# Three stacked transformer blocks: weights asked for one stage ahead, and block three's condition finished inside the last feed-forward step in column tiles

## The chip, the core and the metric

The kernel runs on one core of a Trainium2 chip, written directly against the five engines: TensorE (PE, matrix products, with its weight loads shown as PEld), VectorE (DVE), ScalarE (ACT), GpSimd (POOL) and SyncE (SP). SP and POOL issue transfers to 16 DMA engines that all queues share. The metric is the device time of one launch in microseconds, the median of the timed runs. All data are 32-bit floats.

## The reference, cut to what matters

Three blocks follow one another on x, 256 tokens of width 1024. Block one is attention and 32 experts; block two is a hybrid layer whose one wide input product `x @ w_in_2` has 8192 columns; block three has two layers, each of a feed-forward part, a mixer and a second feed-forward part:

```python
c_act = jax.nn.silu(c)
for i in range(2):
    mod = (c_act @ mod_w[i] + mod_b[i])[:, None, :]
    sh0, sc0, g0, sh1, sc1, g1, sh2, sc2, g2 = jnp.split(mod, 9, axis=-1)
    h = rms_norm(x, norm_g[i, 0]) * (1 + sc0) + sh0
    x = x + 0.5 * g0 * swiglu(h, ffn_w_gu[i, 0], ffn_w_down[i, 0])
    h = rms_norm(x, norm_g[i, 1]) * (1 + sc1) + sh1
    y = pool_mixer(h, pool_w, pool_scale) if i == 0 else diff_attention(h, ...)
    x = x + g1 * y
    h = rms_norm(x, norm_g[i, 2]) * (1 + sc2) + sh2
    x = x + 0.5 * g2 * swiglu(h, ffn_w_gu[i, 1], ffn_w_down[i, 1])
return rms_norm(x, final_g)
```

`swiglu(h)` is `(silu(h @ w_g) * (h @ w_u)) @ w_down` with 2816 inner columns. `mod`, the condition, is nine pieces of 1024 columns a layer.

## The kernel before

The program is a row of stages. A stage holds its tiles and semaphores, and its `block()` gives each engine its own instruction list. All engines meet at the end of a block, so a stage's first transfers are issued when the stage before has ended on every engine.

**Block two** (`second`, line 1618) multiplies w_in_2 in a ring of two slots of 512 columns. SP loads the first two slots at lines 1669 to 1670 and reloads a slot at line 1684 when its last bank is filled. Beside it `SideSums` (line 279) computes the first three pieces of layer 0's condition: POOL loads mod_w in halves of 2 MB (line 299), and DVE adds the rows up, weighted by the condition, with 16 instructions a piece (lines 268 and 272). What results has one partial sum per partition; a product with ones adds the 128 partitions up later.

**A feed-forward stage** (`ffn`, line 2067; ffn00, ffn01 in layer 0, ffn10, ffn11 in layer 1) first runs `Norm`: ACT squares, DVE scales, PE transposes (line 471), DVE and ACT write hT (lines 457, 432). Then come 11 steps of 256 inner columns. `up(s)` makes gate and up products of slot s into banks 4+2s and 5+2s (line 2132), ACT applies silu (line 2175), DVE multiplies (line 2195), `down(s)` adds to banks 0 to 3 (line 2146). Weights lie in two slots: SP loads 2 MB of gate and up weights (lines 2097, 2098) when the slot's second bank is filled, then 1 MB of down weights (line 2101) after the slot's last down product. The order on PE is written out: up 0, up 1, down 0, four turns of (up 0, down 1, up 1, down 0), up 0, down 1, down 0. `residual` (line 2214) then multiplies by the gate and adds to x on DVE. ffn00 carries six pieces of side sums, ffn01 nine; POOL's mod_w loads (2 MB each) run beside SP's weights.

**A modulation stage** (`modulation`, line 331, called by `modulation3`) follows ffn00 with two parts (mixer and second feed-forward of layer 0) and ffn01 with three. PE turns shift and scale sums into columns with 128x1 products (line 382), and gates into rows with 128x512 products (line 390). DVE adds the biases, and folds in the norm's gain, the factor 0.5 or pool_scale.

**The mixers**: `pool_mixer` (line 2226) needs 1 MB of weights; `diff_attention` (line 2308) loads 8 MB of q and k weights (wqk), small tables, lamrow last, and 4 MB of v weights at its start (lines 2338 to 2344). PE waits for wqk and all the tables before its first product (line 2370).

`third` (line 2633) calls these in order.

## Time and profile before

| | |
|---|---|
| timed runs | 3047.74 us median of 3 (3039.37 to 3050.79) |
| profiled execution | 3042.34 us, span 3040.7 us |
| PE busy | 2671.5 us, 88% of the span |
| PE weight loads busy | 1588.9 us, 52% |
| DVE, ACT, POOL busy | 783.5, 336.9, 29.7 us |
| mean granted clock of PE | 0.917 |
| read from memory | 727.83 MB, 240 GB/s over the span |

### The profile page before, as it was taken

The numbers are of one execution on the slowest core, as the hardware profiler recorded it, in microseconds if no ns is written. First come the engines' busy times: TensorE is split into PE (matmuls) and PEld (weight loads), VectorE is DVE, ScalarE is ACT, GpSimd is POOL, SyncE is SP. The second block draws the span as 40 slices with busy tenths as digits, with TensorE's granted clock in tenths as the row PEclk, the third lists the DMA queues.
The fourth block names the chain that finished last, engine by engine and source line by source line (L and its number), as shares of the span: only waits on it lengthen the run. The fifth ranks groups of instructions, "written<-read, shape, count | busy, mean of one in ns | idle before, by whom it ended". The sixth has DMA issues, their size and how long they took to land. (4 is left out here: it accounts for less than half of the span.)

```text
span 3040.7 us, 28745 instructions
## 1 busy us (share of the span) xinstructions
PE 2671.5 (88%) x10935; PEld 1588.9 (52%) x10936; DVE 783.5 (26%) x1801; ACT 336.9 (11%) x663; POOL 29.7 (1%) x48
## 2 busy tenths in 40 slices
PE   6977699999997999968999799959998996957998
PEld 3433333333332333337787477647767774734775
DVE  1222322212121221232832243234441001232001
ACT  2111011111111111110122000010001000021000
POOL 0000000000000000000000000000000000000000
PEclk8967699999999999989999899969997997967999
DMA  7600599999998899966323477347963545102443
GB/s 296 242 0 2 229 419 428 428 429 428 428 428 342 349 428 428 428 265 234 139 100 149 152 288 260 111 148 259 354 225 132 166 154 196 57 1 83 152 136 105
DMA packets 188107, 729.65 MB, mean 240 GB/s; under 512 B 9343, under 2 KB 102877, under 8 KB 159381
## 3 DMA queue, kind: packets, MB, share of 16 engines
q1 hardware_dynamic: 169044, 653.41, 54.7%
q0 software_dynamic: 19008, 75.50, 6.5%
q8 instruction: 36, 0.59, 0.1%
q14 instruction: 19, 0.15, 0.0%
HBM read 727.83 MB, written 1.05 MB: 240 GB/s over the span
## 5 line engine op out<-in xcount | busy, mean ns | idle before, releaser
L2132 PE MATMUL bank<-hT,ffn_wgu 128*128 128x256 f32 x2816 | 622.3, 382 | 29.1 <-DMA ffn_wgu<-in_ffn_w_gu 25.8
L2132 PEld LDWEIGHTS bank<-hT,ffn_wgu 128*128 128x128 f32 x2816 | 538.7, 192 | 123.1 <-issue 42.8
L1387 PE MATMUL bank<-experts_raw,tiled_xs 128*64 128x512 f32 x2112 | 474.3, 599 | 17.4 <-DMA experts_raw<-in_w_up 13.6
L1387 PEld LDWEIGHTS bank<-experts_raw,tiled_xs 128*64 128x64 f32 x2112 | 147.8, 138 | 333.3 <-issue 295.1
L2146 PE MATMUL bank<-ffn_wd,ffn_actT 128*128 128x512 f32 x704 | 308.6, 592 | 0.0
L1387 PE MATMUL bank<-experts_raw,tiled_act_s 128*64 128x512 f32 x1056 | 241.0, 602 | 48.4 <-DMA experts_raw<-in_w_down 47.1
L1714 PE MATMUL bank<-hT,second_ring 128*128 128x256 f32 x1024 | 226.1, 384 | 17.2 <-DMA second_ring<-in_w_in 17.2
L1714 PEld LDWEIGHTS bank<-hT,second_ring 128*128 128x128 f32 x1024 | 197.4, 193 | 46.1 <-issue 18.5
L2195 DVE TENSOR_TENSOR ffn_actT<-ffn_silu,bank 128x256 f32<-128x256 f32 x88 | 36.9, 421 | 694.1 <-ACT ffn_silu L2175 694.1
L2146 PEld LDWEIGHTS bank<-ffn_wd,ffn_actT 128*128 128x128 f32 x704 | 133.8, 190 | 151.3 <-issue 149.2
L1387 PEld LDWEIGHTS bank<-experts_raw,tiled_act_s 128*64 128x64 f32 x1056 | 71.3, 137 | 196.1 <-issue 123.5
L272 DVE SCALAR_TENSOR_TENSOR layer_sums<-ffn_side_w,cact,layer_sums 128x512 f32 (+1 forms) x210 | 140.6, 746 | 3.4 <-DMA ffn_side_w<-in_mod_w 3.4
L2175 ACT ACTIVATE ffn_silu<-bank 128x256 f32<-128x256 f32 x88 | 33.8, 384 | 851.6 <-PE bank L2132 851.6
L1523 DVE COPY tiled_spread<-bank 128x256 f32<-128x256 f32 x33 | 14.0, 425 | 433.9 <-PE bank L1423 433.7
L1554 DVE TENSOR_TENSOR tiled_up<-bank,tiled_cur 128x512 f32<-128x512 f32 x33 | 22.8, 692 | 252.9 <-PE bank L1407 252.9
L2370 PE MATMUL bank<-hT,diff_wqk 128*128 128x256 f32 x256 | 59.1, 392 | 16.6 <-DMA diff_lamrow<-in_diff_lambda 16.6
L1432 PE MATMUL bank<-tiled_ys,tiled_spread 64*128 64x512 f32 x264 | 65.6, 615 | 0.8 <-ACT tiled_ys L1478 0.8
L1415 PE MATMUL bank<-tiled_h_rows,tiled_choice 128*64 128x512 f32 x272 | 65.9, 606 | 0.0
L2370 PEld LDWEIGHTS bank<-hT,diff_wqk 128*128 128x128 f32 x256 | 50.5, 198 | 24.3 <-issue 16.9
L1482 ACT ACTIVATE tiled_g_rows<-bank 128x512 f32<-128x512 f32 x33 | 19.7, 598 | 293.6 <-PE bank L1387 293.6
L1938 DVE SCALAR_TENSOR_TENSOR second_pT<-second_glu,cols,second_pT 128x256 f32<-128x256 f32 x120 | 47.6, 477 | 0.0
L1485 ACT ACTIVATE tiled_u_rows<-bank 128x512 f32<-128x512 f32 x33 | 19.7, 598 | 224.9 <-PE bank L1387 224.9
(460 smaller groups left out, 1974.2 us busy)
## 6 DMA issues: line engine op xcount, KB each, us to landing
experts_raw<-in_w_gate SPq DMA_DIRECT2D x64, 2048.0 KB, 23.7
experts_raw<-in_w_up SPq DMA_DIRECT2D x64, 2048.0 KB, 25.1
experts_raw<-in_w_down SPq DMA_DIRECT2D x64, 2048.0 KB, 25.5
ffn_wgu<-in_ffn_w_gu SPq DMA_DIRECT2D x88, 1024.0 KB, 9.8
ffn_side_w<-in_mod_w POOLq DMA_DIRECT2D x30, 2048.0 KB, 12.0
ffn_wd<-in_ffn_w_down SPq DMA_DIRECT2D x44, 1024.0 KB, 5.2
second_ring<-in_w_in SPq DMA_DIRECT2D x16, 2048.0 KB, 7.7
mla_wm<-in_w_mod SPq DMA_DIRECT2D x24, 1024.0 KB, 6.4
```

What stands on the lines that cost most here:

```text
L272: op = vec.scalar_tensor_tensor(dst[:, o], src[:, j, o], c[:, j:j + 1], dst[:, o], ALU.mult, ALU.add)
L1387: last = nc.tensor.matmul(bank[b][h * HALF:(h + 1) * HALF, :], stationary(kt), raw[p][:, k, h * C:(h + 1) * C], start=kt == 0, stop=kt == ...
L1415: last = nc.tensor.matmul(bank[X][n * HALF:(n + 1) * HALF, :], choice[:, t, :], h_rows[:, t, n * C:(n + 1) * C], start=t == 0, stop=t == T ...
L1432: nc.tensor.matmul(bank[2 * t + h][:], spread[rows, t * P:(t + 1) * P], ys[rows, :], start=False, stop=False)
L1554: vec.tensor_tensor(tiles(up), turned(U), wide(cur[:, KT:2 * KT]), ALU.add).then_inc(u_taken, 1)
L1714: last = nc.tensor.matmul(bank[b][:, (f % 2) * SEQ:(f % 2 + 1) * SEQ], w_k[s][:, k, f * P:(f + 1) * P], core.hT[:, k, :], start=k == 0, st ...
L1938: op = vec.scalar_tensor_tensor(dst, src, w, dst, ALU.mult, ALU.add)
L2132: last = nc.tensor.matmul(bank[b][:, m * SEQ:(m + 1) * SEQ], wgu[:, s, m, k, f * P:(f + 1) * P], core.hT[:, k, :], start=k == 0, stop=k == ...
L2146: last = nc.tensor.matmul(bank[b][:], actT[:, s, f, t * P:(t + 1) * P], wd[:, s, f, n * 512:(n + 1) * 512], start=start and f == 0, stop=s ...
L2175: nc.scalar.activation(silu[:, b - 4, :], core.bank[b][:, 0:SEQ], ACT.Silu)\
L2195: vec.tensor_tensor(actT[:, s, f, :], silu[:, b - 4, :], core.bank[b][:, SEQ:], ALU.mult)\
L2370: last = nc.tensor.matmul(bank[q % 4][:, f * SEQ:(f + 1) * SEQ], wqk[:, k, a:a + P], core.hT[:, k, :], start=k == 0, stop=k == KT - 1)
```

## The change

Four things, all in the second and third block.

1. The ring of block two, one large tile `big` (block two's pT, then both weight slots of all feed-forward stages, then the attention's v weights and q/k), and the semaphores of their loads live across stages.
2. Loads are issued in the stage before: the first w_in slots behind the last expert weights; ffn00's first two steps in block two after `mixed`; ffn01's and ffn10's in the last step of the feed-forward stage before (`following`); wqk at ffn10's start (`early`); ffn11's in the attention after the v products. The slot order changes with the stage (`slots`).
3. The modulation stages are gone. The bias row is added by the side sums, on one partition (others zero). The last step of ffn00 and ffn01 makes, per part, the two column pieces as four rows in 32-column tiles of one bank and the gate as rows, between the last up and down product; ACT copies them out; four transposes per part turn the rows into columns; DVE finishes them. POOL applies pool_scale.
4. `ffn10` and `ffn11` keep their normalised x in the ring; so does the attention for v, probabilities and x.

```diff
+    def first_w_in_2(self, sp):
+        w_in = self.ins["w_in_2"].rearrange("(k p) n -> p k n", p=P)
+        for s in range(2):
+            sp.dma_start(self.ring[:, s, :].rearrange("p (k n) -> p k n", k=KT), w_in[:, :, s * 512:(s + 1) * 512])\
+                .then_inc(*self.slot_in[s].up())
...
-            if first and j == 0:
+            if first and j == 0 and bias is not None:
+                op = vec.scalar_tensor_tensor(dst[:, o], src[:, j, o], c[:, j:j + 1], bias[:, o], ALU.mult, ALU.add)
+            elif first and j == 0:
...
+        if self.bias is not None:
+            self.st.nc.gpsimd.memset(self.bias[:], 0.0).then_inc(*self.zeroed.up())
+            pool.wait_ge(*self.zeroed.own())
+        load_bias(slice(self.first * PIECE, (self.first + 1) * PIECE))
...
             for s in range(2):
                 pool.wait_ge(*self.w_used[s].next(pool))
+                if s == 0:
+                    load_bias(bass.ds(i * PIECE + (self.first + 1) * PIECE, PIECE))
                 load(s, bass.ds(i * PIECE + (self.first + 1) * PIECE, PIECE))
...
@@ experts_tiled, sync
             load(E - 1, 2)
+            core.first_w_in_2(sp)
@@ second, sync
-            for s in range(2):
-                sp.dma_start(w_k[s], w_in[:, :, s * 512:(s + 1) * 512]).then_inc(*slot_in[s].up())
...
+            sp.wait_ge(*S["mixed"].next(sp, 4))
+            core.ffn_weights.first_steps(sp, 0, 0)
...
+class FfnWeights:
+    def slots(layer, which):
+        return (0, 1) if which == 0 else (1, 0)
...
+    def first_steps(self, sp, layer, which):
+        for n, s in enumerate(self.slots(layer, which)):
+            self.load_gu(sp, layer, which, s, self.step(n))
+            self.load_wd(sp, layer, which, s, self.step(n))
...
@@ ffn, sync
-            for s in range(2):
-                load_gu(s, lambda o: slice(o + s * F, o + (s + 1) * F))
-                load_wd(s, lambda o: slice(o + s * F, o + (s + 1) * F))
+            if early:
+                early(sp)
...
+            if following:
+                sp.wait_ge(*core.filled[5 + 2 * B].next(sp))
+                weights.load_gu(sp, *following, B, weights.step(0))
+                sp.wait_ge(*wd_used.next(sp))
+                weights.load_wd(sp, *following, B, weights.step(0))
+                sp.wait_ge(*core.filled[5 + 2 * A].next(sp))
+                weights.load_gu(sp, *following, A, weights.step(1))
+                sp.wait_ge(*core.filled[3].ahead(2))
+                weights.load_wd(sp, *following, A, weights.step(1))
...
@@ ffn, tensor
-            up(0)
-            down(1)
-            down(0, stop=True)
...
+            up(A)
+            if finish:
+                pe.wait_ge(*side.step.next(pe, (2 * KT - 2) * side.n_pieces))
+                pe.wait_ge(*side.w_used[1].next(pe, side.n_pieces))
+            n = 0
+            for part, *_ in finish:
+                a = (3 * part - side.first) * PIECE
+                core.claim(pe, b_of(n))
+                for g in range(4):
+                    last = nc.tensor.matmul(bank[b_of(n)][32 * g:32 * g + 32, :], core.ones[:, 0:32],
+                                            sums[:, a + g * 512:a + (g + 1) * 512], start=True, stop=True)
+                last.then_inc(*core.filled[b_of(n)].up())
+                n += 1
+                for h in range(2):
+                    o = a + 2 * PIECE + h * 512
+                    core.claim(pe, b_of(n))
+                    nc.tensor.matmul(bank[b_of(n)][:], core.ones[:], sums[:, o:o + 512], start=True, stop=True)\
+                        .then_inc(*core.filled[b_of(n)].up())
+                    n += 1
+            down(B)
+            core.copied(pe, *spare_banks[:2 * len(finish)])
+            for i in range(len(finish)):
+                core.claim(pe, b_of(n))
+                for j in range(4):
+                    last = nc.tensor.transpose(bank[b_of(n)][:, j * P:(j + 1) * P], cond_rows[i][:, j * P:(j + 1) * P],
+                                               core.ident[:])
+                last.then_inc(*core.filled[b_of(n)].up())
+                n += 1
+            down(A, stop=True)
...
@@ diff_attention, sync
-            sp.dma_start(wqk[:], w[:, :, 0:2 * D]).then_inc(*qk_in.up())
...
+            for b in (6, 7):
+                sp.wait_ge(*core.filled[b].ahead(TT))
+            core.ffn_weights.first_steps(sp, 1, 1)
...
@@ third
             sums = s0.sb("sums", [P, 6 * PIECE])
-            ffn(core, 0, 0, *part(0, 0), (w[0], 3, 6, sums))
-            modulation3(core, 0, [1, 2], 3, sums)
+            ffn(core, 0, 0, *part(0, 0), (w[0], 3, 6, sums, b_row(0)), following=(0, 1),
+                finish=[(1, 0, core.gate3[1], core.ins["pool_scale_3"]), (2, 0, core.gate3[2], None)])
...
-            ffn(core, 0, 1, *part(0, 2), (w[1], 0, MODS3, sums))
-            modulation3(core, 1, [0, 1, 2], 0, sums)
-        ffn(core, 1, 0, *part(1, 0))
-        diff_attention(core, *part(1, 1))
+            ffn(core, 0, 1, *part(0, 2)[0:2], last_gate[:], (w[1], 0, MODS3, sums, b_row(1)), following=(1, 0),
+                finish=[(n, 1, core.gate3[n], None) for n in range(3)])
...
+            ffn(core, 1, 0, *part(1, 0), early=load_qk)
+            diff_attention(core, wqk, qk_in, *part(1, 1))
```

The order of instructions on SP from the last expert weights to block two, before:

```order
L1262 DMA experts_raw<-in_w_down 128x4096 x2
L175 UNCONDITIONAL_BRANCH
L1600 UNCONDITIONAL_BRANCH
L1602 DMA experts_out_post<-in_norm_ffn_post 128x1024
L175 UNCONDITIONAL_BRANCH
L1667 UNCONDITIONAL_BRANCH
L1670 DMA second_ring<-in_w_in 128x8x512 x2
```

And the same place on SP in the changed kernel:

```order
L1228 DMA experts_raw<-in_w_down 128x4096 x2
L150 DMA ring<-in_w_in 128x8x512 x2
L186 UNCONDITIONAL_BRANCH
L1569 UNCONDITIONAL_BRANCH
L1571 DMA experts_out_post<-in_norm_ffn_post 128x1024
```

The two ring loads now stand ahead of two ends of blocks. On PE, the end of ffn00, the modulation stage and the start of the pool mixer, before:

```order
L2132 MATMUL bank<-hT,ffn_wgu 128x256 x32
L2146 MATMUL bank<-ffn_wd,ffn_actT 128x512 x16
L175 UNCONDITIONAL_BRANCH
L376 UNCONDITIONAL_BRANCH
L382 MATMUL bank<-ones,layer_sums 128x1 x32
L390 MATMUL bank<-layer_sums,ones 128x512 x4
L175 UNCONDITIONAL_BRANCH
L2256 UNCONDITIONAL_BRANCH
L471 MATMUL bank<-ident,pool_xn 128x128 x16
```

And PE at the same place in the changed kernel (`big` is the weights' tile, `ffn_cond_rows` what ACT copied):

```order
L2152 MATMUL bank<-hT,big 128x256 x32
L2193 MATMUL bank<-layer_sums,ones 32x512 x4
L2200 MATMUL bank<-layer_sums,ones 128x512 x2
L2193 MATMUL bank<-layer_sums,ones 32x512 x4
L2200 MATMUL bank<-layer_sums,ones 128x512 x2
L2166 MATMUL bank<-big,ffn_actT 128x512 x8
L2208 MATMUL bank<-ident,ffn_cond_rows 128x128 x8
L2166 MATMUL bank<-big,ffn_actT 128x512 x8
L186 UNCONDITIONAL_BRANCH
L2329 UNCONDITIONAL_BRANCH
L437 MATMUL bank<-ident,pool_xn 128x128 x16
```

The 32 products of one column are gone, the four of 512 moved up, and eight products of 32 columns and eight transposes came in. ffn01 has the same with three parts.

## Rows read from the trace of the kernel before

**Rows 1.** Busy time by stretch, around the two modulation stages (first line: columns)
```profile
core 0: us, PE busy (x) PEld busy (x) DVE busy (x) ACT busy (x) POOL busy (x), PEclk, DMA share, GB/s
...
1972.00:2000.00 28.00, 19.58 (x75) 15.77 (x76) 8.35 (x20) 3.67 (x6) 0.24 (x2) 0.60 0.35 112
...
2279.00:2321.00 42.00, 31.13 (x125) 26.21 (x124) 12.48 (x31) 5.73 (x11) 0.00 (x0) 0.63 0.33 116
```

**Rows 2.** Waits of PE: line and releaser, us in total, times, longest
```profile
PE bank L2132 <- DMA ffn_wgu<-in_ffn_w_gu: 25.8, 10, 9.7
PE bank L1714 <- DMA second_ring<-in_w_in: 17.2, 2, 9.4
PE bank L2370 <- DMA diff_lamrow<-in_diff_lambda: 16.6, 1, 16.6
```

**Rows 3.** Timeline, experts' end and block two: start, length, engine, line, idle before
```profile
1301.57 5.22 SPq L1262 DMA_DIRECT2D experts_raw<-in_w_down  x2
...
1341.86 0.66 ACT L430 ACTIVATE hT<-bank 128x256 f32<-128x256 f32 x2 [0.19 <-PE bank L471]
...
1349.66 29.50 PE L1714 MATMUL bank<-hT,second_ring 128*128 128x256 f32 x128 [7.83 <-DMA second_ring<-in_w_in]
1388.57 58.15 PE L1714 MATMUL bank<-hT,second_ring 128*128 128x256 f32 x256 [9.41 <-DMA second_ring<-in_w_in]
```

**Rows 4.** Timeline, starts of ffn00, ffn01, ffn10 and ffn11
```profile
1722.80 3.68 PE L471 MATMUL bank<-ident,ffn_xn 128*128 128x128 f32 x16 [11.30 <-DVE ffn_xn L447]
1735.79 29.28 PE L2132 MATMUL bank<-hT,ffn_wgu 128*128 128x256 f32 x128 [9.32 <-DMA ffn_wgu<-in_ffn_w_gu]
...
2032.60 3.42 PE L471 MATMUL bank<-ident,ffn_xn 128*128 128x128 f32 x16 [6.08 <-DVE ffn_xn L447]
2045.68 29.64 PE L2132 MATMUL bank<-hT,ffn_wgu 128*128 128x256 f32 x128 [9.66 <-DMA ffn_wgu<-in_ffn_w_gu]
...
2318.93 1.93 ACT L432 ACTIVATE hT<-bank,cond_mod 128x256 f32<-128x256 f32 x4 [4.56 <-PE bank L471]
...
2321.23 27.87 PE L2132 MATMUL bank<-hT,ffn_wgu 128*128 128x256 f32 x128 [1.82 <-ACT hT L432]
...
2794.49 3.67 PE L471 MATMUL bank<-ident,ffn_xn 128*128 128x128 f32 x16 [6.09 <-DVE ffn_xn L447]
2799.64 29.83 PE L2132 MATMUL bank<-hT,ffn_wgu 128*128 128x256 f32 x128 [1.48 <-ACT hT L432]
```

**Rows 5.** Timeline, start of the differential attention
```profile
2556.11 3.67 PE L471 MATMUL bank<-ident,diff_xn 128*128 128x128 f32 x16 [7.16 <-DVE diff_xn L447]
...
2576.34 16.72 PE L2370 MATMUL bank<-hT,diff_wqk 128*128 128x256 f32 x64 [16.56 <-DMA diff_lamrow<-in_diff_lambda]
```

**Rows 6.** Timeline, last residual instruction of ffn00, first instruction of the pool mixer
```profile
1972.30 0.69 DVE L2223 TENSOR_TENSOR x<-x,ffn_xn 128x512 f32<-128x512 f32 x1
...
1994.06 1.06 ACT L419 ACTIVATE pool_xn<-x 128x1024 f32<-128x1024 f32 x1 [35.83 <-PEq L175]
```

**Rows 7.** Timeline, last side sums and end of ffn01, first instruction of ffn10
```profile
2245.68 9.36 DVE L272 SCALAR_TENSOR_TENSOR layer_sums<-ffn_side_w,cact,layer_sums 128x512 f32 x14
...
2251.40 14.08 PE L2132 MATMUL bank<-hT,ffn_wgu 128*128 128x256 f32 x64 [0.44 <-DMA ffn_wgu<-in_ffn_w_gu]
...
2279.97 0.69 DVE L2223 TENSOR_TENSOR x<-x,ffn_xn 128x512 f32<-128x512 f32 x1
...
2310.66 1.06 ACT L419 ACTIVATE ffn_xn<-x 128x1024 f32<-128x1024 f32 x1 [44.77 <-PEq L175]
```

**Rows 8.** Timeline: block one's 32-column products, one down product, one bank's copy
```profile
29.62 2.78 PE L548 MATMUL bank<-mla_wm,first_cpad 128*32 128x512 f32 x24 [0.95 <-ACT mla_ctx_hT L430]
...
2348.93 7.03 PE L2146 MATMUL bank<-ffn_wd,ffn_actT 128*128 128x512 f32 x16
...
1398.51 0.60 ACT L1850 ACTIVATE second_pT<-bank 128x512 f32 x1 [18.61 <-PE bank L1714]
```

**Rows 9.** Reload of block two's ring, and the stretch until it lands
```profile
1365.53 14.20 SPq L1684 DMA_DIRECT2D second_ring<-in_w_in  x2
...
1365.00:1389.00 24.00, 14.59 (x67) 12.57 (x66) 12.46 (x22) 1.80 (x3) 2.44 (x4) 0.89 1.03 395
```

More of the change, by code:

```diff
@@ L134, in __init__, with hold @@
         self.cact = sb("cact", [P, KT])
+    def hold(self, name, shape):
+        return self.ctx.enter_context(self.nc.sbuf_tensor(name, shape, F32, side="right"))
     def clear_signals(self):
@@ L279, with __init__ @@
 class SideSums:
-    def __init__(self, st, w, first, n_pieces, acc, n_turns, slot=None):
+    def __init__(self, st, w, first, n_pieces, acc, n_turns, slot=None, bias=None):
         self.st, self.rows, self.acc, self.first = st, KT // 2, acc, first
@@ L293, in __init__ @@
         self.step = st.sem("side_step")
-        self.turn = [(x, self.per_turn) for x in self.w_in + self.w_used] + [(self.step, (2 * KT - 2) * self.per_turn)]
+        self.b_row, self.bias = bias, None
+        self.b_in, self.zeroed = st.landed("side_b_in"), st.sem("side_zeroed")
+        if bias is not None:
+            self.bias = st.sb("side_bias", [P, PIECE])
+        self.loads = self.w_in + ([self.b_in] if bias is not None else [])
+        self.turn = [(x, self.per_turn) for x in self.loads + self.w_used] + [(self.step, (2 * KT - 2) * self.per_turn)]
     def gpsimd(self, pool):
@@ L2070, in ffn @@
+def ffn(core, layer, which, scale, shift, gate, beside=None, following=None, early=None, finish=()):
     nc, ins = core.nc, core.ins
-    F = 256
+    F = FfnWeights.F
     steps = DFF3 // F
+    weights = core.ffn_weights
+    wgu, wd, gu_in, wd_in = weights.wgu, weights.wd, weights.gu_in, weights.wd_in
+    A, B = weights.slots(layer, which)
     with Stage(core, f"ffn{layer}{which}") as st:
-        wgu = st.sb("wgu", [P, 2, 2, KT, F])
-        wd = st.sb("wd", [P, 2, 2, D])
         actT = st.sb("actT", [P, 2, 2, SEQ])
@@ L2084, in ffn @@
+        cond_rows = [st.sb(f"cond_rows{i}", [P, 512]) for i in range(len(finish))]
+        pool_row = st.sb("pool_row", [P, D]) if any(own is not None for *_, own in finish) else None
+        pool_row_in, raw_gate, gate_done = st.landed("pool_row_in"), st.sem("raw_gate"), st.sem("gate_done")
+        spare_banks = (4 + 2 * B, 5 + 2 * B)
+        b_of = lambda n: spare_banks[n % 2]
+        sums = beside and beside[3]
         block = st.block()
@@ L2578, in _ @@
                                   subln[:], None, ALU.mult).then_inc(*core.emptied[q].up())
-            residual(core, dve, gate, wv, step)
+            residual(core, dve, gate, junk, step)
 def final_norm(core):
@@ L2619, in _ @@
                                                ALU.mult, ALU.mult).then_inc(*done.up())
-def modulation3(core, layer, parts, first, sums):
-    ins, b_mod = core.ins, core.ins["mod_b_3_row"]
-    at = layer * MODS3
-    own = [0.5, ins["pool_scale_3"] if layer == 0 else 1.0, 0.5]
-    gain = lambda n: core.column("norm_g_3", (layer * 3 + n) * KT, KT)
-    modulation(core, f"mod3{layer}{first}",
-               [(3 * n + m, gain(n) if m else None, core.mod3[:, layer, 2 * n + m, :]) for n in parts for m in range(2)],
-               [(3 * n + 2, b_mod[(at + 3 * n + 2) * D:(at + 3 * n + 3) * D], own[n], core.gate3[n][:]) for n in parts],
-               lambda piece: core.column("mod_b_3", (at + piece) * KT, KT), first, sums)
 def third(core):
```

238 lines of the change are left out of this document (124 added, 114 removed).

## The prediction

> **What bounds the kernel now.** The table of stretches was read first, then the list of what TensorE (PE) waited for, then the timeline at each border between stages. Nearly everywhere PE is the bound: in a feed-forward step 64 instructions of the up product and 16 of the down product follow one another without a gap. The loss is at the borders. In the stretch around the first modulation stage PE is busy 19.6 of 28 us at a granted clock of 0.60, around the second 31.1 of 42 us at 0.63 [rows 1]. The waits for transfers that can be moved are 25.8 us for feed-forward weights in 10 waits, 17.2 us for block two's weights in 2, and 16.6 us at the start of the differential attention in one [rows 2]. So I price the change border by border, as the time from the last instruction that stays to the first that stays.
>
> **Block two's first weights.** The SP queue issues the last expert weights by 1301.57 + 5.22 = 1306.8 us; the change puts the first two w_in loads right behind. They are 4.2 MB, 10.6 us at the 395 GB/s of [rows 9], and block two is more than 30 us away. hT is complete at 1341.86 + 0.66 = 1342.5; in ffn10 the first product follows the last hT write by 2321.23 - 2320.86 = 0.4 us [rows 4], so here it can start at 1342.9. It started at 1349.66 [rows 3]. **Saved 6.8.**
>
> The second wait of block two is another matter. The reload of slot 0 was issued at 1365.53 and PE got it at 1388.57, 23 us later, after 9.41 us of waiting, while the DMA engines were full and moved 395 GB/s [rows 3, 9]: the side loads of mod_w from the POOL queue compete. The change takes 4.2 MB, 10.6 us of work, out of what is ahead, but PE also asks 6.8 us earlier. Net 3.8 us, so the wait falls from 9.4 to 5.6. **Saved 3.8**, the least certain term. Its ends: all of the wait, with the 2.5 us that the products behind it lose to the low clock (estimated from the 2.0 us loss found below); or nothing, with the 6.8 us above given back as a longer wait.
>
> The Trainium skill (DMA: Bandwidth & Descriptors, "Queues, rings and completion order") says that each DMA engine takes turns between its queue rows, packet by packet. With even turns the reload would get about half of the rate, land in 10.6 us and cause no wait at all. The row with its 23 us speaks against even turns here; this is the rival "no second wait" below.
>
> **First feed-forward steps.** With weights present, a stage's first up product starts 2799.64 - 2794.49 = 5.15 us after its transposes start [rows 4]. The stage ffn00 took 1735.79 - 1722.80 = 12.99, the stage ffn01 13.08 [rows 4]. **Saved 7.8 and 7.9.** ffn10 (1.82 us wait for ACT, not for weights) and ffn11 gain nothing. In ffn00 the loads now follow the "mixed" wait and run beside the output product of block two; in ffn01 they run beside the last step and the pool mixer.
>
> **Differential attention.** PE started 2576.34 - 2556.11 = 20.2 us after its transposes, held by the small tables that sat behind 8 MB of wqk [rows 5]. wqk now lands during ffn10, so 5.15 us should do: 15.1 saved. The first 64 instructions took 16.72 us against half of 27.87 at full clock [rows 4, 5], a loss of 2.8; behind a 1.48 us wait the 128 of ffn11 lose 29.83 - 27.87 = 2.0 [rows 4], so 0.8 more. **Saved 15.9.** The 8 MB go ahead of ffn10's loop loads on the SP queue. They take 21 us from the start of the stage; the first loop load is asked for after 2321.23 - 2310.66 = 10.6 us of norm [rows 4, 7] plus 14 us of up product. I cost this at nothing. Without that cover it is one wait of some us.
>
> **The modulation stages.** The first: the last residual instruction ends 1972.30 + 0.69 = 1972.99, the pool mixer's first ACT instruction is at 1994.06 [rows 6]; a stage follows another's last instruction by 0.3. Removed 20.8. The second: 2279.97 + 0.69 = 2280.66 to 2310.66 [rows 7], removed 29.7.
>
> Added instead, per part, between the last up product and the down products: four products of 32 columns of ones, two rows of 512, and later four transposes. Block one has the same 32-column form, 24 instructions (three sets of four) in 2.78 us, 0.93 a set; a full 128x512 instruction takes 7.03 / 16 = 0.44, four of them 1.76; 16 transposes take 3.67, four 0.92 [rows 4, 8]. That is 3.6 a part. PE uses two banks in turn while ACT copies each in 0.60 [rows 8] plus a handover near 0.3; against 0.88 to 0.93 per bank that hides but for some tenths, 0.5 a stage. So 2 x 3.6 + 0.5 = 7.7 and 3 x 3.6 + 0.5 = 11.3. **Saved 13.1 and 18.4.** ffn10 pays one thing back: its first 128 instructions ran at full clock (27.87) behind the modulation's products; now they follow an idle stretch, as in ffn11 (29.83), so -2.0 and **16.4** is left. The cost of a part could be higher: 4 x 0.88 instead of 0.93 if the four column tiles ran one after another (+2.6), and 3 x 0.9 if each bank waited for ACT (+2.7), 26.5 us over five parts. Nothing excludes a small gain below, but no row suggests one.
>
> The new waits. PE waits for the sums: the last piece ends at 2245.68 + 9.36 = 2255.0, PE needs it at 2251.40 + 14.08 = 2265.5 [rows 7], 10 us of slack. Behind that wait on PE are both down products, so a late piece would cost one for one. The bias makes two DVE instructions a piece longer, 0.69 us each at most [rows 6], inside the same slack. The four or six small DVE writes of the columns lie under the last down product of 7 us. The multiply by pool_scale on POOL starts when its gate is copied and has two down products, 14 us, as cover; no row here shows it, DVE's two-input instruction of half the width takes 0.69 [rows 6]. The Trainium skill (GPSIMD Engine Reference, "Elementwise — side-by-side cycle accounting") has 4.5 us for twice the width, an estimate of 2.2 us here, which changes nothing.
>
> **Sum.** 6.8 + 3.8 + 7.8 + 13.1 + 7.9 + 16.4 + 15.9 = 71.7 us. The profiled execution took 3042.3 (span 3040.7), so 2970.6. It lies 5.4 below the median of the three timed runs and between their ends, so the same may hold after.
>
> **Rivals.**
> *No second wait* in block two: the reload lands in time. The 5.6 and 2.5 us go too: 2962.5. For it: 10.6 us less transfer work. Against: the 23 us for one load.
> *The start is given back*: side loads set the pace of DMA in block two, the reload lands when it did before, less nothing. PE's 6.8 and the 3.8 are lost: 2981.2. For it: full DMA from 1365 to 1389 [rows 9].
> *Condition work in series* on PE, with the column tiles not overlapped and ACT in every bank's turn: +26.5, 2997.1. Against: the 0.93 us of [rows 8].
> *The change doesn't do what it says*: SP reaches the early loads only at the border, because it waits in order on its queue. Then 6.8 + 3.8 + 7.8 + 7.9 + 15.9 = 42.2 stay: 3012.8. Against: each wait ahead of them is on a bank that PE fills 7 us or more before the end; only the last wd load waits for the very end.
> *Slower*: side loads crowd out weights inside ffn00 and ffn01. There are 16 loop loads of gate and up weights beside them. Now the waits there are 25.8 - 9.32 - 9.66 = 6.8 in 8 [rows 2, 4]. Were each to wait the 9.41 us of block two's reload, that is 150 us: 2970.6 + 150 - 7 = 3114. It beats the gain from (71.7 + 15) / 16 = 5.4 us a load. Against: bytes, order and slack per load stay as they are; only 4 KB of bias a piece are new.
>
> **How the numbers follow.** Forecast 0.58, no second wait 0.15, start given back 0.12, condition in series 0.06, loads not early 0.06, slower 0.03. The likeliest is 2971. The low end is 2962.5 less the 6.8 us of small weight waits, 2956. The high end is 2981.2 and 10 us more, for half of the 11.4 us between the runs and a partial overlap in the condition work: 2991. The first three cases are inside, 0.85. A measurement of this kernel tells about 0.5%, 15 us, from no change. All cases but the last are faster by more than that: faster 0.96; same 0.01 for a mixture; slower 0.03.
>
> **What would show it.** Right: no stage of modulation, PE's wait for ffn weights near 7 instead of 25.8, no wait for lamrow, first products 5.1 to 5.2 us after the transposes in ffn00, ffn01 and the attention, a piece of condition work of 7 to 8 and 11 us in the last steps, and one wait of 4 to 7 us for block two's ring. Wrong: a new wait of PE for layer_sums, waits on the spare banks longer than 1 us, a wait in ffn10's first steps behind wqk, or a span above 2991.

## The result, and the profile after

| | before | after |
|---|---|---|
| timed runs | 3046.93 us median of 4 (3039.37 to 3050.79) | 2964.32 us median of 4 (2961.74 to 2967.82) |
| profiled span | 3040.7 us | 2966.3 us |
| PE busy | 2671.5 us | 2641.4 us |
| mean granted clock of PE | 0.917 | 0.931 |

The ratio is 0.9733, 95% interval 0.9711 to 0.9754. The forecast was 2971 us with a range of 2956 to 2991. The span fell by 74.4 us, where the terms of the prediction summed to 71.7.

The main waits of PE after the change, line and releaser, us in total, times, longest:

```profile
PE bank L1354 <- DMA experts_raw<-in_w_down: 47.0, 43, 14.8
...
PE bank L437 <- DVE ring L413: 20.4, 3, 7.2
PE bank L437 <- DVE ffn_xn L413: 17.7, 2, 11.4
...
PE bank L2340 <- DVE hT L2374: 13.7, 1, 13.7
...
PE bank L2152 <- DMA big<-in_ffn_w_gu: 8.8, 7, 2.3
```

The 25.8 us for feed-forward weights [rows 2] have become 8.8, and the longest of these waits 2.3 instead of 9.7. The wait for lamrow is gone. The head of the list is the experts' down weights in block one, 47.0 us against 47.1 before. In the third block what is left is mostly DVE's arithmetic, at the borders (the L413 rows) and in the mixers. The change touches neither.

The timeline of PE after the change, one row for each place named below: start, length, engine, line, tiles, shape, count, idle time before.

```profile
1343.52 29.48 PE L1683 MATMUL bank<-hT,ring 128*128 128x256 f32 x128 [1.14 <-ACT hT L396]
1375.71 55.52 PE L1683 MATMUL bank<-hT,ring 128*128 128x256 f32 x256 [2.71 <-DMA ring<-in_w_in]
...
1709.63 3.67 PE L437 MATMUL bank<-ident,ffn_xn 128*128 128x128 f32 x16 [11.41 <-DVE ffn_xn L413]
1714.79 29.86 PE L2152 MATMUL bank<-hT,big 128*128 128x256 f32 x128 [1.48 <-ACT hT L398]
...
1924.63 11.17 PE L2152 MATMUL bank<-hT,big 128*128 128x256 f32 x51
1935.73 1.06 PE L2193 MATMUL bank<-layer_sums,ones 128*32 128x512 f32 x8
1936.73 1.99 PE L2200 MATMUL bank<-layer_sums,ones 128*128 128x512 f32 x4
1938.64 1.07 PE L2193 MATMUL bank<-layer_sums,ones 128*32 128x512 f32 x8
1939.64 1.98 PE L2200 MATMUL bank<-layer_sums,ones 128*128 128x512 f32 x4
1942.40 7.11 PE L2166 MATMUL bank<-big,ffn_actT 128*128 128x512 f32 x16 [0.78 <-ACT third_gate L2238]
1949.34 1.04 PE L2208 MATMUL bank<-ident,ffn_cond_rows 128*128 128x128 f32 x8
1950.21 7.03 PE L2166 MATMUL bank<-big,ffn_actT 128*128 128x512 f32 x16
1964.41 3.67 PE L437 MATMUL bank<-ident,pool_xn 128*128 128x128 f32 x16 [7.17 <-DVE pool_xn L413]
...
1996.82 3.68 PE L437 MATMUL bank<-ident,ffn_xn 128*128 128x128 f32 x16 [6.28 <-DVE ffn_xn L413]
2002.00 29.61 PE L2152 MATMUL bank<-hT,big 128*128 128x256 f32 x128 [1.50 <-ACT hT L398]
...
2255.76 3.67 PE L437 MATMUL bank<-ident,ring 128*128 128x128 f32 x16 [7.17 <-DVE ring L413]
2260.91 29.86 PE L2152 MATMUL bank<-hT,big 128*128 128x256 f32 x128 [1.47 <-ACT hT L398]
...
2497.78 3.68 PE L437 MATMUL bank<-ident,ring 128*128 128x128 f32 x16 [7.16 <-DVE ring L413]
2502.89 16.23 PE L2446 MATMUL bank<-hT,diff_weights_wqk 128*128 128x256 f32 x64 [1.43 <-issue]
...
2725.11 29.86 PE L2152 MATMUL bank<-hT,big 128*128 128x256 f32 x128 [1.48 <-ACT hT L398]
```

Two things are read from it. The first is the lead: the start of a piece before [rows 3 to 5] minus its start after. It grows where time was won, so its steps are the measured terms. They also carry what differs between two executions: of the 0.7 us that the first step is short, 0.6 lies ahead of it, where PE began the transposes at 1338.74 instead of 1338.18.

| up to | lead | step | predicted |
|---|---|---|---|
| block two, first product | 6.1 | 6.1 | 6.8 |
| block two, end of the ring's first products | 15.5 | 9.3 | 3.8 |
| ffn00, transposes | 13.2 | -2.3 | 0 |
| ffn00, first product | 21.0 | 7.8 | 7.8 |
| ffn01, transposes | 35.8 | 14.8 | 13.1 |
| ffn01, first product | 43.7 | 7.9 | 7.9 |
| ffn10, transposes | 60.3 | 16.6 | 18.4 |
| attention, transposes | 58.3 | -2.0 | -2.0 |
| attention, first product | 73.5 | 15.1 | 15.1 |
| ffn11, first product | 74.5 | 1.1 | 0.8 |
| end | 74.4 | -0.1 | 0 |

The second is the condition inside ffn00. The last up product ends at 1924.63 + 11.17 = 1935.80, the down product starts at 1942.40: 6.6 us. The transposes between the down products add 1950.21 - 1949.34 = 0.87. That is 7.5 us, predicted 7.7, of which 0.78 is a wait that was not predicted. Four 32-column products (eight instructions) advance PE by 1936.73 - 1935.73 = 1.00 us, against 1.91 for two full rows. In ffn01 the same reading gives 10.9, predicted 11.3.

### The profile page after: what moved, and what is told of

It reads as the page before. It is cut to its first block and busy times, and to the rows that moved or that the text cites. A ratio compares the mean times of both kernels' runs of the same rounds, so it can differ in the third digit from the quotient of the medians.

```text
span 2966.3 us, 28580 instructions
## 1 busy us (share of the span) xinstructions
PE 2641.4 (89%) x10835; PEld 1557.5 (53%) x10836; DVE 779.6 (26%) x1776; ACT 345.6 (12%) x678; POOL 43.2 (1%) x67
## 5 line engine op out<-in xcount | busy, mean ns | idle before, releaser
L2152 PE MATMUL bank<-hT,big 128*128 128x256 f32 x2816 | 623.3, 383 | 14.7 <-DMA big<-in_ffn_w_gu 8.8
L2152 PEld LDWEIGHTS bank<-hT,big 128*128 128x128 f32 x2816 | 539.9, 192 | 108.9 <-issue 24.7
L2166 PE MATMUL bank<-big,ffn_actT 128*128 128x512 f32 x704 | 309.1, 592 | 1.5 <-ACT third_gate L2238 1.5
L1683 PE MATMUL bank<-hT,ring 128*128 128x256 f32 x1024 | 224.3, 382 | 3.8 <-DMA ring<-in_w_in 2.7
L2166 PEld LDWEIGHTS bank<-big,ffn_actT 128*128 128x128 f32 x704 | 133.6, 190 | 153.2 <-issue 151.3
L1683 PEld LDWEIGHTS bank<-hT,ring 128*128 128x128 f32 x1024 | 196.5, 192 | 32.5 <-issue 5.7
L285 DVE SCALAR_TENSOR_TENSOR layer_sums<-ring,cact,layer_sums 128x512 f32 (+1 forms) x210 | 140.6, 745 | 2.8 <-DMA ring<-in_mod_w 2.8
L2446 PE MATMUL bank<-hT,diff_weights_wqk 128*128 128x256 f32 x256 | 58.7, 390 | 1.4 <-issue 1.4
L2446 PEld LDWEIGHTS bank<-hT,diff_weights_wqk 128*128 128x128 f32 x256 | 50.1, 196 | 9.0 <-issue 1.8
L1907 DVE SCALAR_TENSOR_TENSOR big<-second_glu,cols,big 128x256 f32<-128x256 f32 x120 | 47.6, 479 | 0.0
## 6 DMA issues: line engine op xcount, KB each, us to landing
ring<-in_mod_w POOLq DMA_DIRECT2D x30, 2048.0 KB, 11.9
```

Source lines behind the costliest of these rows:

```text
L285: op = vec.scalar_tensor_tensor(dst[:, o], src[:, j, o], c[:, j:j + 1], dst[:, o], ALU.mult, ALU.add)
L1683: last = nc.tensor.matmul(bank[b][:, (f % 2) * SEQ:(f % 2 + 1) * SEQ], w_k[s][:, k, f * P:(f + 1) * P], core.hT[:, k, :], start=k == 0, st ...
L1907: op = vec.scalar_tensor_tensor(dst, src, w, dst, ALU.mult, ALU.add)
L2152: last = nc.tensor.matmul(bank[b][:, m * SEQ:(m + 1) * SEQ], wgu[:, s, m, k, f * P:(f + 1) * P], core.hT[:, k, :], start=k == 0, stop=k == ...
L2166: last = nc.tensor.matmul(bank[b][:], actT[:, s, f, t * P:(t + 1) * P], wd[:, s, f, n * 512:(n + 1) * 512], start=start and f == 0, stop=s ...
L2446: last = nc.tensor.matmul(bank[q % 4][:, f * SEQ:(f + 1) * SEQ], wqk[:, k, a:a + P], core.hT[:, k, :], start=k == 0, stop=k == KT - 1)
```

## The experiments

Three places were open: how much each half of the change carries, the reload wait of block two (predicted 5.6, measured 2.71), and the clock at the starts of stages.

### Each half alone

**own_start** keeps the condition inside the last steps and puts every load back to the start of its own stage.

```diff
             load(E - 1, 2)
-            core.first_w_in_2(sp)
...
-            if early:
-                early(sp)
+            weights.first_steps(sp, layer, which)
...
         def _(sp):
+            load_qk(sp)
             for i, name in enumerate(("cos3", "sin3")):
```

> The condition work stays inside the last feed-forward steps; all weights are again asked for at their own stage's start. If the gain is a sum of borders, the trace of the change says what comes back: 6.1 us at block two's first product, 6.7 at its reload and about 2.6 of low clock behind it, 7.8 at ffn00, 7.9 at ffn01, 15.6 at the attention, 46.7 in all: 3011 us, with waits for weights of 9.3 and 9.7 us in ffn00 and ffn01 and 16.6 for lamrow. If early loads and condition work hide one another (rival), less than 40 comes back, and with mod_stages the two do not add up to the 82 us between the medians.

Measured: 3005.22 us, ratio 0.9878 (0.9857 to 0.9899). Timeline of PE in this kernel:

```profile
1350.50 30.23 PE L1681 MATMUL bank<-hT,ring 128*128 128x256 f32 x128 [8.39 <-DMA ring<-in_w_in]
...
1735.95 30.34 PE L2149 MATMUL bank<-hT,big 128*128 128x256 f32 x128 [7.32 <-DMA big<-in_ffn_w_gu]
...
2018.53 3.68 PE L437 MATMUL bank<-ident,ffn_xn 128*128 128x128 f32 x16 [6.28 <-DVE ffn_xn L413]
2026.31 30.23 PE L2149 MATMUL bank<-hT,big 128*128 128x256 f32 x128 [4.11 <-DMA big<-in_ffn_w_gu]
...
2540.03 15.57 PE L2441 MATMUL bank<-hT,diff_weights_wqk 128*128 128x256 f32 x64 [15.79 <-DMA diff_lamrow<-in_diff_lambda]
```

Each wait is back at its place, but the time fell short of the 46.7 us and the 3011 us expected. The early loads are worth 0.9878 - 0.9733, 1.45% or 44 us, with some 9 of uncertainty, and 36 between the two traces. Two starts came out shorter than before the change: ffn01's first product comes 7.8 us after the transposes start, not 13.1, and ffn00's 11.0, not 13.0 [rows 4]. In both stages POOL issues its first side load 1.8 and 2.8 us behind SP's first weights, where it was 0.5 before, since the new memset and bias load stand ahead of it. That this is why the weights land sooner was not tested. Another 2.0 us are ffn10's first 128 products, 27.87 us in this trace and 29.86 in that of the change.

**mod_stages** keeps the early loads and puts the two modulation stages back. They add the bias as they did before, and the side sums leave it out.

```diff
-                finish=[(1, 0, core.gate3[1], core.ins["pool_scale_3"]), (2, 0, core.gate3[2], None)])
+            modulation3(core, 0, [1, 2], 3, sums)
...
-                finish=[(n, 1, core.gate3[n], None) for n in range(3)])
+            modulation3(core, 1, [0, 1, 2], 0, sums)
```

> Early loads stay; the two modulation stages are back and the bias rows leave the side sums. Sum of borders: 13.1 and 18.7 us come back, less 2.0 because ffn10's first products run at full clock again: 29.8 us, 2994 us. If the clock gain of ffn10 was an accident of when the stage starts (rival), its first 128 instructions take 29.8 instead of 27.9 and 31.8 us come back.

Measured: 2988.86 us, ratio 0.9828 (0.981 to 0.9846). That puts the condition's move at 0.95%, 29 us with some 9 of uncertainty, for 29.8 expected. The two spans differ by 21.4 us only; 2.9 of the rest lie ahead of block two's first product, where the kernels are the same. Timeline of PE:

```profile
2245.31 17.50 PE L413 MATMUL bank<-ones,layer_sums 128*128 128x1 f32 x96 [1.78 <-PEq L186]
2262.67 6.94 PE L421 MATMUL bank<-layer_sums,ones 128*128 128x512 f32 x12
2277.32 3.68 PE L502 MATMUL bank<-ident,ring 128*128 128x128 f32 x16 [7.71 <-DVE ring L478]
2282.48 29.73 PE L2217 MATMUL bank<-hT,big 128*128 128x256 f32 x128 [1.48 <-ACT hT L463]
```

The second expectation missed. The modulation stands right ahead of ffn10 again, but ffn10's first 128 take 29.73 us and not 27.9. What sets the length of those products is taken up under the clock, below.

The gains are also to be read from the kernel before: early loads alone (mod_stages) give 1.72%, 52 us, the condition alone (own_start) 1.22%, 37 us. Together that is 89 where both give 2.67%, 81 us. The 8 us between them are not clear of the noise, some 11 us for three ratios. The traces point the same way: own_start has ffn00's and ffn01's starts 2.0 and 5.3 us shorter than before the change, so that much of the two starts is won by either half.

### Does the column form matter

**one_group** puts all four 32-column products of a part in the same group of columns; it leaves out rows two to four of each shift and scale.

```diff
-                    last = nc.tensor.matmul(bank[b_of(n)][32 * g:32 * g + 32, :], core.ones[:, 0:32],
+                    last = nc.tensor.matmul(bank[b_of(n)][0:32, :], core.ones[:, 0:32],
```

> All four products of a set go to the first 32 columns, so rows two to four of a set are left out of the result (shift and scale of block three are wrong in part). If the column tiles of the change run side by side, a set grows from 1.07 us to 4 x 0.88 = 3.5, five sets cost 12.2 us: 2976 us. If they already ran one after another (rival), nothing changes.

Measured: 2976.84 us, ratio 0.9791 (0.9773 to 0.981). Timeline of PE in ffn00's last step:

```profile
1932.33 3.62 PE L2193 MATMUL bank<-layer_sums,ones 128*32 128x512 f32 x8
1935.88 1.99 PE L2200 MATMUL bank<-layer_sums,ones 128*128 128x512 f32 x4
```

The same eight instructions take 3.62 us in one group of columns and 1.07 in four. Over five parts that is 12.8 us, and the ratio rose by 0.6%, 18 us, with some 9 of uncertainty. So the first half of the rival "condition in series", 2.6 us a part, was a real price, and the column groups are what avoids it. Its other half, a wait for ACT at each bank, is absent from the timeline of the change, but for the 0.78 us.

**no_bias** leaves the condition's bias out of the sums.

```diff
-            ffn(core, 0, 0, *part(0, 0), (w[0], 3, 6, sums, b_row(0)), following=(0, 1),
+            ffn(core, 0, 0, *part(0, 0), (w[0], 3, 6, sums, None), following=(0, 1),
...
-            ffn(core, 0, 1, *part(0, 2)[0:2], last_gate[:], (w[1], 0, MODS3, sums, b_row(1)), following=(1, 0),
+            ffn(core, 0, 1, *part(0, 2)[0:2], last_gate[:], (w[1], 0, MODS3, sums, None), following=(1, 0),
```

> The bias of block three's condition is left out: no bias rows, no memset, the first side-sum instruction one-input again. ffn01 loses 4.5 us to waits for weights in the change against 2.7 before. If the small bias loads on the POOL queue are the reason, the waits fall to 2.7 and the time by about 2 us. If it is the moment at which the side loads start (rival), they stay near 4.5 and the time within 1 us of the change.

Measured: 2957.78 us, ratio 0.9733 (0.9711 to 0.9755), the same as with the bias. ffn01's four weight waits came to 3.7 us, against 4.5 with it, 2.7 before the change and 2.1 in mod_stages. The bias rows cost nothing that can be told; where ffn01's 2 us went stays open.

### The small waits that were left

**after_again** and **after_third** are the changed kernel unedited, on the chips of the second and the third group of runs.

> The changed kernel once more, unedited, as the measure for the three runs beside it: 0.9733 of the time of the kernel before. It also tells how far the rows move without any edit: the first 128 gate and up products of a stage take 27.9 us where the granted clock came back to full before them and 29.9 us where it came back after they had begun, and which of the two a stage gets may differ from the first profile (29.9 in ffn00, 29.6 in ffn01, 29.9 in ffn10, 29.9 in ffn11).

> The changed kernel a third time, beside the two runs that follow, so that they are compared on one chip: 0.973 of the kernel before, as twice before (0.9733 and 0.9728).

Measured: 0.9728 (0.9714 to 0.9743) and 0.975 (0.9733 to 0.9767); medians 2964.24 and 2965.42 us.

**copied_first** moves one wait.

```diff
             up(A)
+            core.copied(pe, 4 + 2 * B, 5 + 2 * B)
...
-            down(B)
+            down(B, wait=False)
```

> In both feed-forward steps that hold the condition, the wait for the last down product's two banks stands ahead of the condition's products instead of behind them. My theory: the 0.78 and 0.73 us that TensorE waits there for ScalarE's copy of a condition tile are an accident of how evictions are counted (the counter takes in the tile's copies) and not a need, so both rows go and nothing else moves: 1.5 us less, a ratio of 0.9728. The rival: the down product's own banks were emptied late too, and a wait for VectorE of about the same length takes the place: 0.9733, no change.

Measured: 2960.79 us, ratio 0.973 (0.9716 to 0.9743). In the trace the down product follows the condition without a gap:

```profile
1942.51 1.98 PE L2202 MATMUL bank<-layer_sums,ones 128*128 128x512 f32 x4
1944.33 7.03 PE L2167 MATMUL bank<-big,ffn_actT 128*128 128x512 f32 x16
```

Both rows are gone and no other wait came in their place. 1.5 us is below what the ratio can tell.

**reload_first** holds the third block's later side loads until the reload has landed.

```diff
+        if self.hold is not None:
+            pool.wait_ge(*self.hold)
         with turns(pool, self.n_pieces - 1, *[(x, 1) for x in self.loads + self.w_used]) as i:
...
+        side.hold = slot_in[0].ahead(2)
```

> In block two the third and later pieces that GpSimd loads for the third block's condition are held until the reload of the first slot has landed. My theory: the reload lands late (16.3 us after its issue, TensorE 2.71 us idle) because it shares the DMA engines with these pieces; held back, they leave the reload to land within about 10 to 12 us, before the other slot's products end, so the wait of 2.71 us goes, and the clock does not fall there; VectorE's side work comes some 15 us later and still ends long before it is read. 3 to 5 us less than the changed kernel (0.9717 to 0.9723). The rival: the two packets before it are already in flight and carry the delay, or the clock's dip comes from elsewhere: the wait stays above 2 us, no change.

Measured: 2964.45 us, ratio 0.9745 (0.9732 to 0.9759). Timeline, POOL's queue and PE:

```profile
1363.61 1.48 POOL L317 DMA_DIRECT2D second_wb<-in_mod_w  x2 [25.22 <-DMA ring<-in_w_in]
...
1397.88 12.35 PE L1686 MATMUL bank<-hT,ring 128*128 128x256 f32 x56 [0.92 <-DMA ring<-in_w_in]
```

The reload, issued at 1355.32, landed within 7.4 us instead of 16.2; POOL goes on at 1363.61. The wait of 2.71 is gone, a later one of 0.92 has come. From block two's first product to ffn00's transposes the trace has 1703.67 - 1341.06 = 362.6 us against 1709.63 - 1343.52 = 366.1. So the cause of the wait is right, contention with POOL's loads. The timed runs show no gain of it (0.9745 against 0.9728, intervals that overlap), and the same stretch is 359.4 us in after_third, unedited (1708.72 - 1349.31).

The traces of seven other executions, whose kernels leave this place as the change has it, say when the wait appears. First SP's reload and POOL's side load nearest to it in the timeline of the changed kernel, and the time from issue to landing (last number, us) of the reload alone; then the same two views of after_third:

```profile
1358.16 0.74 POOL L317 DMA_DIRECT2D second_wb<-in_mod_w  x1 [17.31 <-DVE second_wb L285]
...
1359.37 14.20 SPq L1651 DMA_DIRECT2D ring<-in_w_in  x2
```

```profile
ring<-in_w_in SPq DMA_DIRECT2D x1, 2048.0 KB, 16.2
```

```profile
1363.57 0.39 SPq L1651 DMA_DIRECT2D ring<-in_w_in  x1
...
1364.77 0.74 POOL L317 DMA_DIRECT2D second_wb<-in_mod_w  x1 [18.12 <-DVE second_wb L285]
```

```profile
ring<-in_w_in SPq DMA_DIRECT2D x1, 2048.0 KB, 10.2
```

In five traces (the first one after, after_again, copied_first, no_bias, mod_stages) POOL's load was issued 1.0 to 1.5 us before the reload: it landed after 15.9 to 16.9 us, and PE waited 2.4 to 3.4. In four (after_third, one_group, fill, fill2) it was issued 1.0 to 1.2 us behind it: 9.8 to 11.0 us, and no wait. The order of two issues a microsecond apart can differ between executions of one kernel: the three traces of the unedited change have it one way twice and the other way once. The nine traces sort cleanly by the order, but no run sets it on purpose, and why it is worth 5 us or more is open.

### The clock at the starts of stages

**fill** issues products that nobody reads, in PE's idle time ahead of the transposes; they are added work and replace nothing.

```diff
+        for _ in range(fill):
+            nc.tensor.matmul(core.bank[7][:, 0:P], core.ones[:], core.ident[:], start=True, stop=True)
         if self.normalise:
...
-            norm.tensor(pe)
+            norm.tensor(pe, {(0, 0): 44, (0, 1): 24, (1, 0): 28, (1, 1): 24}[layer, which])
```

> Products of the ones with the identity, 128 columns each, into a bank that nobody reads, are issued in TensorE's wait ahead of the transposes of the four feed-forward steps and of the attention (44, 24, 28, 24 and 28 of them, worked out at 0.21 us each from 27.86 us for 128 products of 256 columns). They add no useful work. My theory: the granted clock falls to half in these waits and comes back only during or after the transposes, which costs 2 us in the first 128 products (29.86 against 27.86) and 2.2 us in the attention's first 64 (16.23 against 14.05), and up to 1.8 us in each set of 16 transposes (3.67 us at half clock). With TensorE busy there the clock stays at full, the first products take 27.9 and 14.05, and the kernel gets 10 to 19 us faster than the changed one: ratio 0.967 to 0.970. The rival: the clock falls all the same (it follows something else than TensorE's idle time), or the added products hold up the transposes by as much: 0.9733 or above.

Measured: 2965.62 us, ratio 0.9751 (0.9737 to 0.9764), no gain. The profile is of its fastest execution, 2955.20 us, but what makes it fast lies ahead of the added products: from the moment ffn00's normalised x is ready to the end it has 1256.2 us, where the unedited kernel has 1256.7 and 1256.0 (first trace and after_third). Busy time and granted clock in ffn01's start (columns: us, PE busy, PEclk, DMA share, GB/s):

```profile
1990.00:1991.00 1.00, 0.81 (x8) 1.00 1.02 418
1991.00:1992.00 1.00, 0.00 (x0) 1.00 0.98 406
1992.00:1993.00 1.00, 0.29 (x1) 1.00 1.07 434
1993.00:1994.00 1.00, 1.00 (x4) 0.55 1.02 410
```

The clock is full through the transposes, which take 1.91 us instead of 3.68, and then falls behind the next gap, the 1.9 us in which PE waits for hT. The first 128 products took 29.55 us in ffn01, ffn10 and ffn11; only ffn00's (27.86) and the attention's 64 (14.05) ran at full clock. So in three of five stages the first fill moved the fall instead of removing it.

That is not the main reason why fill gained nothing. Its added products ran past the waits: DVE's last write to ffn00's normalised x ends at 1695.90 + 1.55 = 1697.45, and the transposes start only at 1704.43, 7.0 us late, where the unedited kernel starts them at once. The other four stages lose 1.0 to 1.2 us each in the same way, 11 us in all. So the clock gave back about as much as the added products cost: the mechanism of the expectation holds, and so does the second half of its rival. These are the rows of DVE and PE in ffn00:

```profile
1695.90 1.55 DVE L413 TENSOR_SCALAR ffn_xn<-x,ffn_small 128x1024 f32<-128x1024 f32 x2
...
1704.43 1.91 PE L439 MATMUL bank<-ident,ffn_xn 128*128 128x128 f32 x16
```

**fill2** fills both gaps with counts that fit: fewer products ahead of the transposes (17 instead of 44 in ffn00, where the transposes are now 2.4 us late, and in the other stages not at all), and 6 behind them. It also fills two waits of the pool mixer (22 and 44 products), which fill left open.

```diff
+            norm.tensor(pe, {(0, 0): 17, (0, 1): 18, (1, 0): 22, (1, 1): 17}[layer, which], 6)
...
             last.then_inc(*core.filled[b].up())
+        self.fill(pe, after)
         core.copied(pe, 0, 1, 2, 3)
...
+            norm.fill(pe, 44)
             pe.wait_ge(*w_in.next(pe))
```

> The idle products once more, with counts that fit: the first trace with them shows 0.23 to 0.26 us for each and not 0.21, with 1.8 us (7.0 before ffn00) until the first one is issued, so that 24 and 28 of them ran past the wait by 0.7 to 1.2 us; and it shows the clock falling after the transposes instead, in the 1.9 us in which TensorE waits for ScalarE's copies, in three of five stages (ffn01, ffn10, ffn11: first 128 products still 29.5). Now 17, 18, 22, 22 and 17 stand ahead of the transposes, 6 behind them, and 22 and 44 in the pool branch's two waits. My theory: the clock stays at full through both gaps, so that the transposes take 1.9 instead of 3.67 us, the first products 27.9 instead of 29.9 and the attention's 14.05: 3 to 4 us in each of five stages and some 3 in the pool branch, 15 to 22 us less than the changed kernel, ratio 0.966 to 0.968. The rival: what the clock gives back in these places the chip takes elsewhere, or the timed runs have it by themselves as often as not (as the first fill's 2965.6 against 2964.2 says): 0.972 to 0.974.

Measured: 2950.94 us, ratio 0.9705 (0.9688 to 0.9721), against 0.975 (0.9733 to 0.9767) of the changed kernel on the same chip: 14.5 us between the medians, and intervals that do not touch. The profile is of the fastest execution, 2946.19 us. From ffn00's normalised x to the end it has 1242.8 us, 13 to 14 less than the kernels above. The timeline of PE at the attention, and then busy time and clock around it (columns as above):

```profile
2477.80 5.15 PE L430 MATMUL bank<-ident,ones 128*128 128x128 f32 x44 [1.78 <-PEq L186]
2483.19 1.97 PE L443 MATMUL bank<-ident,ring 128*128 128x128 f32 x16 [0.24 <-DVE ring L413]
2484.99 1.50 PE L430 MATMUL bank<-ident,ones 128*128 128x128 f32 x12
2487.01 14.05 PE L2454 MATMUL bank<-hT,diff_weights_wqk 128*128 128x256 f32 x64 [0.51 <-issue]
```

```profile
2474.00:2482.00 8.00, 6.22 (x42) 1.00 0.22 54
2482.00:2490.00 8.00, 7.25 (x51) 1.00 0.92 368
```

In the changed kernel the same border has 0.50 for the 8 us from 2495, and 16.23 instead of 14.05. Here the first product starts 3.8 us after the transposes do, before it was 5.1. The gain fell just short of the 15 to 22 us expected. fill2 differs from fill in three things at once, and no run parts them. Read from the traces, the counts take back 8.7 of fill's 11 us; three stages' first 128 products fall from 29.55 to 27.86 us, 5.1 us, behind the 6 added products; and from the pool mixer's transposes to ffn01's it is 29.4 us against 32.4 to 34.0 in the unedited kernel, 3 us or more. One place where some came back is ffn00, whose loads were now late:

```profile
1764.38 14.08 PE L2159 MATMUL bank<-hT,big 128*128 128x256 f32 x64 [0.88 <-DMA big<-in_ffn_w_gu]
...
1788.06 15.76 PE L2159 MATMUL bank<-hT,big 128*128 128x256 f32 x64 [2.73 <-DMA big<-in_ffn_w_gu]
```

The two waits are 3.6 us where the changed kernel has 2.3, and the 64 products behind the second take 15.76 instead of 14.08: 3 us in all.

The Trainium skill (TensorE: Matmul & The Clock Gate, "HAM oscillation — how this bites in real kernels") holds that gaps in TensorE's work let the clock fall. The traces agree: behind the gap of 1.9 us in fill it was 0.55, and in fill2, with 0.24 and 0.51 us left beside the transposes, it stayed at 1.00. The 1.78 us ahead of fill2's first products, at a stage's start, cost no clock.

**best** is fill2, copied_first and reload_first together.

> The three small repairs together: fitted idle products, the down product's bank wait ahead of the condition, and the third block's side loads behind block two's reload. From their traces 1.4 us (the 0.78 and 0.73 rows gone) and 3.5 us (block two's first products to ffn00's transposes: 362.6 instead of 366.1), beside what the idle products give: 20 to 27 us less than the changed kernel if these do what the run before expects, ratio 0.964 to 0.967; 0.971 to 0.973 if only the two others hold.

Measured: 2947.53 us, ratio 0.9683 (0.9667 to 0.9699), 17.9 us under the changed kernel on the same chip and the fastest of all. Its interval overlaps that of fill2, so what the two small repairs add (3.4 us between the medians) isn't shown.

## Why the prediction was right

**The starts** of ffn00, ffn01 and the attention came to the tenth: 7.8, 7.9 and 15.1. The reason is in the method. With weights present, a start is a chain of transposes and copies up to the first product, 5.15 us in ffn11 before [rows 4], and it is 5.16, 5.18 and 5.11 after. own_start brings the waits back, though in ffn00 and ffn01 not in full.

**Block two's start** was 0.7 short (6.1 for 6.8), of which 0.6 lies ahead of the border.

**The reload** was the term that failed in size. "Net 3.8 us, so the wait falls from 9.4 to 5.6" measured 6.7 on the wait (9.41 to 2.71) and 2.6 on the products behind it (58.15 to 55.52 us), which the forecast left out and the rival "no second wait" had at 2.5. The step that was wrong is the subtraction: I took 10.6 us of removed transfer work minus 6.8 of earlier demand. SP issues the reload when PE has filled a bank, 15.87 us after the first product before the change and 15.85 us after it (1365.53 - 1349.66, 1359.37 - 1343.52). So issue and demand moved earlier together, and nothing had to be subtracted: the wait fell by exactly what the landing time fell, 6.7 us (22.9 to 16.2). In the four traces with the reload first the landing time fell by 11.9 to 13.1, and the wait was gone. own_start puts the first loads back to the stage's start, and the reload takes 22.1 us again.

My rival "no second wait", priced at 0.15, is what four of nine traces show. I took the 23 us for one reload as evidence against even turns; with the reload issued first it takes 9.8 to 11.0 us. The sentence of the Trainium skill on packet-by-packet turns (DMA: Bandwidth & Descriptors, "Queues, rings and completion order") gives an estimate of 10.6 us there, and the traces agree; with a side load ahead, 16 us, they do not.

**What I did not count** is a loss of 2.3 us later in block two, where pieces ran at a lower clock, and one of 1.9 us in ffn01, whose weight waits grew from 2.7 to 4.5. They take back most of the reload's surplus of 5.5 us, and 1.7 us won in ffn00 and the pool mixer, not counted either, came in addition. So the sum, 2.7 us off, is closer than its parts, and that is luck.

**The modulation stages** fit: from the end of the last up product to the next stage's transposes 41.7 us became 28.6, and 50.6 became 32.0: 13.1 and 18.6 for 13.1 and 18.4. The cover assumed for the evictions, the POOL multiply (2.34 us, estimated at 2.2) and the sums held; there is no wait for layer_sums. The price of the added work was right by luck in part. I took four transposes at 0.92 us from a row of 16 in 3.67 [rows 4], whose granted clock is 0.50; in the last steps it is full, and eight of them advance PE by 0.87. That is 0.5 us a part too much, and the 0.5 a stage for ACT's copies was not needed. The one new wait, 0.78 and 0.73 us for the third gate's copy, was not foreseen. It comes from a counter: a down product's bank wait now includes the condition's copies. copied_first removes it by order alone.

**ffn10's 2.0 us** was right in number, and its cause is not borne out. I had it pay for the lost modulation products ahead of it. With them back (mod_stages) the first 128 still took 29.73 us. Without them they took 27.9 in own_start, copied_first, no_bias and one_group, and 29.6 to 29.9 in all three traces of the changed kernel and in reload_first. Such a length differs between executions of one kernel: ffn01's was 27.86 in after_third, 29.61 and 29.70 in the other two. So the hit is luck. Only fill2 and best, with the gaps filled, had 27.86 in all four feed-forward stages.

**The other rivals**: "given back" needed the reload to land no earlier, and it did land earlier; "in series" is excluded by one_group, which carries the price of the column tiles, and by the timeline, which has no wait at each bank; "loads not early" and "slower" by the waits (8.8 us in 7).

## What to carry to other kernels

Price a load that is moved ahead by the chain that is left once the data is there, and read that chain from a stage that already has its data: it was right to 0.1 us three times. Ask what sets the moment of an issue before subtracting earlier demand from a wait: where the same engine's progress sets both, they move together. Price a wait in a crowded stretch of transfers as a choice of two values, which here went with the order of two issues, and not by bytes alone. Price an instruction from a row at the clock that it will get. Where an engine's clock falls in short gaps at borders, look at every gap of a border, and fit the number of filling products to the wait. Some 11 us of overrun took back all that the first fill won, and the second, with counts that fit, gained 14.5 us of 2965.

## What the runs showed of the hardware that I had not expected

- A 2 MB reload beside side loads lands after 9.8 to 11.0 us if it is issued 1.0 to 1.2 us ahead of the other queue's load (four traces), after 15.9 to 16.9 if 1.0 to 1.5 us behind it (five), and after 7.4 us with that load held back.
- Executions of one kernel differ by 1.8 us in the same 128 products (ffn01: 27.86, 29.61, 29.70) and by 2.2 us in the attention's 64 (14.05 in after_again, 16.23 in the first trace, 16.18 in after_third), by where the granted clock comes back. One trace's value for a stage start is a sample of two.
- Useless products can pay: fill2 has a median of 2950.94 us against 2965.42 for the unedited kernel beside it, at a mean clock of 0.944 against 0.929 in the profiles.
